# A hybrid MLA and RWKV-7 layer with routed experts: first loads moved a stage early, a folded tail tile, transposed experts of 96 rows, and the slot table made by matmuls

## The reference, cut to what matters

```python
h = rmsnorm(x); p = h @ w_in           # latents | rope key | RWKV columns z (1792) | gate logits (2*1024)
o_a = chunk_causal_attention(q, k, v)  # 8 heads, 96 wide, values 64 wide
o_b = rwkv7_time_mix(z, ...)           # 8 heads of 64: state S = S*w + (S a) b + v k
x = x + sum_n sigmoid(gate_n) * (branch_n @ w_out[n])
h2 = rmsnorm(x)
g = argmax_group(h2); e1, e2 = top2 experts of g     # 4 groups of 8 experts
x = x + sum_k weight_k * ((silu(h2 @ w_gate[e]) * (h2 @ w_up[e])) @ w_down[e])   # D 1024, FF 256
```

## Time and profile before

| | us |
|---|---|
| median of 3 runs (1848.87 to 1853.21) | 1850.72 |
| the profiled execution | 1846.78 |
| its span, first to last instruction | 1845.0 |
| PE busy in it | 1605.4 (87%) |
| DVE / ACT / POOL busy | 883.4 / 450.8 / 110.0 |
| mean granted TensorE clock, as a share of 2.4 GHz | 0.946 |

### The profile page before, as it was taken

How to read it: one execution, slowest core, us unless ns; L and a number is a source line. 1 busy time by engine, 2 the same in 40 slices (tenths; PEclk the granted TensorE clock), 3 DMA queues, 4 the chain that set the end, 5 groups by cost and what they waited for, 6 DMA issues and landing times. The chain is left out here.

```text
span 1845.0 us, 30700 instructions
## 1 busy us (share of the span) xinstructions
PE 1605.4 (87%) x12312; PEld 1037.5 (56%) x12312; DVE 883.4 (48%) x1874; ACT 450.8 (24%) x873; POOL 110.0 (6%) x131
## 2 busy tenths in 40 slices
PE   4999999659999999999994888759981599999994
PEld 3888888525666666666663555525540244444442
DVE  2454645536566666666663666526663122222221
ACT  2222222222222322332211333324540011111110
POOL 0000000000000000000000000000003222222221
PEclk9999999879999999999995999979995799999997
DMA  9322321262231231221104344244526499999982
GB/s 330 118 85 80 113 97 63 83 227 74 71 118 58 78 111 48 78 78 53 59 24 132 102 88 88 64 177 161 201 85 237 148 368 368 365 365 373 373 296 38
DMA packets 103630, 280.20 MB, mean 152 GB/s; under 512 B 31776, under 2 KB 50336, under 8 KB 94032
## 3 DMA queue, kind: packets, MB, share of 16 engines
q1 hardware_dynamic: 93680, 244.78, 37.6%
q0 software_dynamic: 9824, 33.63, 7.2%
HBM read 209.45 MB, written 68.98 MB: 151 GB/s over the span
## 5 line engine op out<-in xcount | busy, mean ns | idle before, releaser
L1069 PE MATMUL b_ps<-b_wg,b_hT 128*128 128x512 f32 x576 | 277.7, 615 | 29.6 <-DMA b_wg<-w_gates 29.3
L1986 PE MATMUL f_hidden<-wgu,f_xT 128*128 128x512 f32 x512 | 225.7, 594 | 0.0
L505 PEld LDWEIGHTS a_ps<-a_hT,a_wz 128*128 128x128 f32 x1792 | 202.6, 192 | 3.8 <-issue 3.8
L505 PE MATMUL a_ps<-a_hT,a_wz 128*128 128x128 f32 x1792 | 204.0, 275 | 0.0
L1069 PEld LDWEIGHTS b_ps<-b_wg,b_hT 128*128 128x128 f32 x576 | 101.4, 191 | 124.7 <-issue 119.9
L1986 PEld LDWEIGHTS f_hidden<-wgu,f_xT 128*128 128x128 f32 x512 | 97.7, 191 | 122.5 <-issue 122.5
L1753 PE MATMUL d_ps<-wo,d_oT 128*128 128x512 f32 x288 | 130.8, 603 | 0.8 <-DVE d_oT L1588 0.8
L2003 PE MATMUL f_down<-wd,f_midT 128*128 128x512 f32 x256 | 116.9, 600 | 1.0 <-DVE f_midT L2023 1.0
L1422 PE MATMUL c_score<-c_kT,c_qT 96*128 96x512 f32 (+2 forms) x192 | 76.2, 508 | 24.5 <-DMA c_v<-v_d 24.5
L2023 DVE COPY f_midT<-f_midps 128x256 f32<-128x256 f32 x32 | 13.6, 425 | 162.7 <-PE f_midps L1993 162.7
L1753 PEld LDWEIGHTS d_ps<-wo,d_oT 128*128 128x128 f32 x288 | 53.4, 192 | 59.4 <-issue 57.8
(11 more groups left out here) (308 smaller groups left out, 2474.6 us busy)
## 6 DMA issues: line engine op xcount, KB each, us to landing
wgu<-w_gate_up SPq DMA_DIRECT2D x32, 2048.0 KB, 13.7
wd<-w_down SPq DMA_DIRECT2D x32, 1024.0 KB, 6.7
b_hT<-hT_d SPq DMA_DIRECT2D x36, 512.0 KB, 4.1
gate_d<-b_logits SPq DMA_DIRECT2D x36, 256.0 KB, 2.6
d_gate<-gate_d SPq DMA_DIRECT2D x9, 1024.0 KB, 5.8
b_wg<-w_gates SPq DMA_DIRECT2D x4, 2048.0 KB, 12.7
zm_d<-a_zm SPq DMA_DIRECT2D x9, 896.0 KB, 4.6
b_zm<-zm_d SPq DMA_DIRECT2D x9, 896.0 KB, 6.5
```

What stands on the lines that cost most here:

```text
L505: mm = pe.matmul(banks[Z_BANKS[n % 2]][:, j * P:(j + 1) * P], wz[:, i, (g + j) * P:(g + j + 1) * P], hT[t % 2][:, i, :], start=(i == 0), s ...
L1069: mm = pe.matmul(banks[FILL][:], hT[q % 2][:, k, :], wg[u % 2][:, k, :], start=(k == 0), stop=(k == DC - 1))
L1986: mm = pe.matmul(hidden[b][:], xT[b][:, k, :], wgu[wb][:, k, :], start=(k == 0), stop=(k == DC - 1))
```

## The change

1. The first loads of a stage are issued by SP in the stage before it, into memory that is kept apart for them: mixing's constants, first zm, hT and gate weights during inputs; attention's first head during mixing; merge's constants and first tile (but the attention output) during attention; the first 3 experts' weights during merge. WB is 5.
2. The folded tail: the gate logits of the last tile use only its 32 real rows, as four matmuls of 32 stationary and 128 moving columns side by side (`QUADS`), in two parts for each unit in place of eight. `FILL_OF` and the fill of s = -1 are changed with it.
3. In mixing, `right_side`, `outputs` and `state` work in halves of 64 stationary columns; `state` computes only the diagonal blocks.
4. Attention takes the tiles in the order 7, 0, 6, 1, 5, 2, 4, 8, 3.
5. merge builds a 96-row table of token numbers and weights with two matmuls per tile, and gathers the first two experts' rows itself. The stage `slots` is gone; the DRAM table is left for overflow alone and is made during the experts' loop, on DVE (eight parts) and POOL (18 indirect DMAs).
6. `CAP` is 96. `up` has the weights as the stationary operand in halves of 64 columns and the rows as 96 moving columns, so its product is already turned and `turn_mid` is gone. OVERFLOW goes from 16 to 22 rounds.

```diff
-CAP = P
+CAP = 96
 OVERFLOW = 2 * (SEQ + DEC) // CAP
-WB = 4
+WB, WB_EARLY = 5, 3
+EARLY = 2
@@ inputs_stage, SP
+            def load_for_mixing():
+                sp.wait_ge(h_stored[0], 16)
+                sp.wait_ge(h_stored[1], 16)
+                sp.wait_ge(zm_stored, 16)
+                for dst, src in mixing_consts(early, io):
+                    sp.dma_start(dst, src).then_inc(early["consts_in"], 16)
+                sp.dma_start(early["zm"][0], io["zm_d"][0]).then_inc(early["zm_in0"], 16)
+                sp.dma_start(early["hT"][0][:], io["hT_d"][0]).then_inc(early["hT_in0"], 16)
+                sp.dma_start(early["wg"][0][:], io["w_gates"][:, :, 0:512]).then_inc(early["wg_in0"], 16)
...
+                if t == NT - 3:
+                    load_for_mixing()
@@ mixing
-        FILL_OF = (3, 2, 3, 3, 3, 2, 4, 4, 2, 1, 2, 3)
+        FILL_OF = (2, 2, 3, 2, 3, 2, 3, 4, 2, 1, 2, 2)
+        QUADS = [slice(DEC * n, DEC * n + DEC) for n in range(P // DEC)]
+        FOLDED = UW // len(QUADS)
+        parts_of = lambda q: DC if tile_of(q) < LAST else 2
...
-            return 2 if s < 0 else FILL_OF[k]
+            return 3 if s < 0 else FILL_OF[k]
@@ mixing, PE, fill
+                        for n, rows in enumerate(QUADS):
+                            mm = pe.matmul(banks[FILL][rows, 0:FOLDED], hT[q % 2][:, k, 0:DEC], wg[u % 2][:, k, n * FOLDED:(n + 1) * FOLDED],
+                                           start=(k == 0), stop=(k == DC - 1), tile_position=(0, DEC * n))
@@ right_side (outputs alike)
-                    pe.matmul(banks[XD][:, p * P:(p + 1) * P], art[t % 2][:, p, 0:P], S[t % 2][:, p, :], start=True, stop=False)
+                    for q in HALVES:
+                        pe.matmul(banks[XD][q, p * P:(p + 1) * P], art[t % 2][:, p, 0:P][:, q], S[t % 2][:, p, :], start=True, stop=False)
@@ state
-                    pe.matmul(banks[XD][:, cols], tok[t % 2][0:real, 1, cols], W[0:real, cols], start=True, stop=False)
+                    for q, cols in heads:
+                        pe.matmul(banks[XD][q, cols], tok[t % 2][0:real, 1, cols], W[0:real, cols], start=True, stop=False)
@@ mixing, SP, s == LAST
+                    load_head(sp, io, early, 0, 0, early["head_in0"])
@@ attention
-        tile_of = lambda p: p % STEPS
+        TILE_ORDER = (NPT - 1, 0, NPT - 2, 1, NPT - 3, 2, NPT - 4, NPT, 3)
+        tile_of = lambda p: TILE_ORDER[p % STEPS]
...
+            for dst, src in ((begun["ident"][:], io["ident"]), (begun["wr"][:], io["w_router"]), (begun["br"][:], io["b_router"].partition_broadcast(P)),
+                             (begun["before"][:], io["causal"][:, 0:P]), (begun["g_ffn"][:], io["norm_ffn_g"].partition_broadcast(P)),
+                             (begun["count_up"][:], io["count_up"].partition_broadcast(P)), (begun["real"][:], io["real"]), (begun["token"][:], io["token"]),
+                             (begun["places"][:], io["places"].partition_broadcast(P)), (begun["nobody"][:], io["nobody"])):
+                sp.dma_start(dst, src).then_inc(keep["begun_in"]["consts"], 16)
+            sp.dma_start(begun["gate0"][:], io["gate_d"][0]).then_inc(keep["begun_in"]["gate"], 16)
@@ merge, SP
+                if 1 <= t <= WB_EARLY:
+                    e = t - 1
+                    sp.dma_start(keep["wgu"][e][:], io["w_gate_up"][ORDER[e]]).then_inc(keep["weights_in"][f"up_in{e}"], 16)
+                    sp.dma_start(keep["wd"][e][:], io["w_down"][ORDER[e]]).then_inc(keep["weights_in"][f"down_in{e}"], 16)
@@ merge, POOL
+            pool.wait_ge(rows_known, 1)
+            for e in range(EARLY):
+                pool.tensor_copy(index[e][:], row_of[:, ORDER[e]:ORDER[e] + 1]).then_inc(index_set, 1)
...
+                pool.indirect_dma_start(xg[e][:], None, io["h2_d"].rearrange("t p n -> (t p) n"),
+                                        bass.IndirectOffsetOnAxis(ap=index[e][:, 0:1], axis=0)).then_inc(keep["gathered"][f"x_in{e}"], 16)
@@ merge, DVE, record
+                if n >= 1:
+                    dve.tensor_tensor(table[:], table[:], banks[7][0:CAP, P:P + 2 * NE], ALU.add)
...
+                dve.tensor_tensor(at_place[:], spread(places[:].unsqueeze(1), [P, 2, CAP]),
+                                  spread(rec[:, 2 * NE + 2:2 * NE + 4].unsqueeze(2), [P, 2, CAP]), ALU.is_equal)
+                dve.tensor_scalar(told[:, :, 0, :], hot(n), token[:, n:n + 1], None, ALU.mult)
+                dve.tensor_tensor(told[:, :, 1, :], hot(n), spread(rec[:, 2 * NE + 4:].unsqueeze(2), [P, 2, NE]),
+                                  ALU.mult).then_inc(told_ready, 1)
@@ merge, PE
+            def place_rows(n):
+                pe.wait_ge(told_ready, n + 1)
+                for k in range(2):
+                    mm = pe.matmul(banks[7][0:CAP, P:P + 2 * NE], at_place[:, k, :], told[:, k], start=(k == 0), stop=(k == 1))
@@ experts, up
-            for k in range(DC):
-                mm = pe.matmul(hidden[b][:], xT[b][:, k, :], wgu[wb][:, k, :], start=(k == 0), stop=(k == DC - 1))
+            for part, flag in enumerate(("gate_done", "up_done")):
+                bank = (gated, upped)[part][b]
+                for f in range(FB):
+                    cols = slice(f * CAP, (f + 1) * CAP)
+                    for k in range(DC):
+                        for half in HALVES:
+                            mm = pe.matmul(bank[half, cols], wgu[wb][:, k, (part * FB + f) * P:(part * FB + f + 1) * P][:, half],
+                                           xT[b][:, k, :], start=(k == 0), stop=(k == DC - 1))
+                mm.then_inc(s[flag], 1)
@@ experts, PE
-                turn_mid(pe, s, e)
                 if e + 2 < NE:
-                    turn(pe, s, e + 2, e % 2, e // 2 + 1)
-                project(pe, s, e, e % WB, e // WB)
+                    turn(pe, s, e + 2, (e + 2) % AHEAD, (e + 2) // AHEAD)
+                project(pe, s, e, e % 2, e % WB, e // WB)
@@ experts, POOL
                 if e + AHEAD < NE:
-                    gather(pool, s, e + AHEAD, e % AHEAD, (e + AHEAD) % (2 * AHEAD), ORDER[e + AHEAD])
+                    gather(e + AHEAD)
+                if 0 <= e - 10 < 2 * NT:
+                    scatter(e - 10)
```

More of the change, by code:

```diff
@@ L561, in _, with mixing @@
                 turn_heads(t)
-def mixing(nc, io):
+def mixing(nc, io, early):
     LEVELS = (2, 4, 8, 16, 32, 64)
@@ L1910, in experts @@
-def experts(nc, io, keep):
-    BLOCKS = NE + OVERFLOW + 2
+            pe.wait_ge(counted, NT)
+            place_rows(NT - 1).then_inc(table_done, 1)
+def experts(nc, io, keep):
+    TRASH = 2 * NT
+    BLOCKS = OVERFLOW + TRASH
+    NBMAX = -(-(SEQ + DEC) // CAP)
     AHEAD = 4
-    ORDER = [g * EPG + e for e in range(EPG) for g in range(NG)]
+    FB = FF // P
+    HALVES = (slice(0, P // 2), slice(P // 2, P))
     with ExitStack() as c:
@@ new lines, in experts @@
+        run, route = keep["run"], keep["route"]
+        slot = sb("slot", [CAP, OVERFLOW, 2])
+        oindex = sb("oindex", [CAP, 1], I32)
+        weight = sb("weight", [CAP, 1])
+        count_up = sb("count_up", [P, NE])
+        trash = sb("trash", [P, NT, 2])
+        token = sb("token", [P, NT])
+        more = sb("more", [P, NE])
+        bounds = sb("bounds", [P, NBMAX - 1])
+        gt = sb("gt", [P, NE, NBMAX - 1])
+        upto = sb("upto", [P, NE])
+        one = sb("one", [P, NE])
@@ new lines, in experts @@
+        base = sb("base", [P, NE])
+        owned = sb("owned", [P, OVERFLOW, NE])
+        q = sb("q", [P, NT, 2])
+        ge = sb("ge", [P, NT, 2, NBMAX - 1])
+        hb = sb("hb", [P, NT, 2, NE])
+        bb = sb("bb", [P, NT, 2])
+        over = sb("over", [P, NT, 2])
+        place = sb("place", [P, NT, 2])
+        entry = sb("entry", [P, NT, 2, 2])
+        cell = [[sb(f"cell{t}_{k}", [P, 1], I32) for k in range(2)] for t in range(NT)]
+        planf = sb("planf", [P, OVERFLOW + 1])
+        plan = sb("plan", [P, OVERFLOW + 1], I32)
@@ L2001, in project @@
             for h in range(2):
-                for k in range(2):
-                    mm = pe.matmul(down[h][:], midT[:, k, :], wd[wb][:, k, 512 * h:512 * h + 512], start=(k == 0), stop=(k == 1))
+                for k in range(FB):
+                    mm = pe.matmul(down[h][0:CAP, :], midT[b][:, k, :], wd[wb][:, k, 512 * h:512 * h + 512], start=(k == 0), stop=(k == FB - 1))
             mm.then_inc(s["down_done"], 1)
@@ L2073, in work @@
                 goes_on(pool, o["add_seen"])
-            pool.wait_ge(slot_in, 16 + START)
-            for e in range(AHEAD):
-                gather(pool, s, e, e, e, ORDER[e])
+            for e in range(EARLY, AHEAD):
+                gather(e)
+            pool.memset(one[:], 1.0).then_inc(one_set, 1)
             for e in range(NE):
```

556 lines of the change are left out of this document (280 added, 276 removed).

## The result

The changed kernel takes 1759.42 us in the median (1758.26 to 1761.13), 0.9506 of before (95% interval 0.949 to 0.9523). The prediction was 1669, with a range from 1634 to 1716: the sign was right, the gain was 91 us where 182 were forecast. The profiled execution spans 1756.4 us, 88.6 less than before.

The account below looks back on a forecast made before the run. The prediction took PE's own work to bound mixing and experts, PE's waits attention, with idle gaps between stages; its terms summed to -181 us, 1846.8 to 1665.8, as a median 1669, range 1634 to 1716.

Parts of the forecast that it names:

- A: Start of mixing: with loads issued during inputs, PE's first matmul comes earlier, -16 us.
- C: Start of attention: with the first head loaded during mixing, PE starts earlier, -6 us.
- E: Start of merge: with constants and first tile already loaded, PE starts earlier, -15 us.
- B: Body of mixing: less fill, and halves side by side in outputs, right_side and state, -45 us.
- D: Attention's tile order: wide next to narrow tiles gives ACT time and cuts PE's waits, -10 us.
- G: Between merge and experts: no slots stage and gathers issued in merge bring PE's first turn earlier, -41 us.
- H: The experts: PE's period falls to 9.73 us with the other work hidden, -56 us.
- R1: Rival in the experts: DMA, not PE, sets the pace, costing 10 to 25 us; chance 22%.
- R2: Rival: DVE's chain takes PE's savings in mixing and attention's order gains nothing, +43 us; chance 12%.
- R3: Rival in the experts' up: a fixed time per instruction bounds small matmuls, +42 us; chance 3%.
- R4: Rival in experts and mixing: the halves don't run side by side, +208 us, slower than before; chance 4%.
- R5: Rival in the experts: an expert overflows its 96 rows and one overflow block runs, about +33 us; chance 4%.

Follow-up runs that it names:

- e3: The changed kernel with mixing's fill batches never running over the end of a unit, same number of matmuls; 1737.83 us, ratio 0.9396.
- e4: The changed kernel with attention's tiles taken in the order 0 to 8 again; 1755.15 us, ratio 0.949.
- e8: The changed kernel with the first two gathers issued at the start of the experts, not in merge, and the identity kept in memory; 1759.73 us.
- e1: The changed kernel with the experts' gathers issued one period earlier, before POOL waits for the output rows; 1738.85 us, ratio 0.94.
- e9: The changed kernel with gathers two periods early, fill ending at unit ends, attention's tiles in order and the identity kept; 96-row gathers and scatters; 1715.18 us.
- e11: The four edits of e9 on the changed kernel, with 128 rows in the gathers and 96 in the scatters; 1690.6 us, ratio 0.914.
- e12: The changed kernel with gathers of 128 rows as the only edit, scatters and PE still at 96; 1736.48 us, ratio 0.9376.
- e7: The changed kernel with gathers a period early and the scatter of each expert's output rows left out; 1698.39 us.
- e5: The kernel before the change, with half of the experts' up and down matmuls left out; 1841.72 us.
- e10: The four edits of e9 on the changed kernel, with 128 rows in both gathers and scatters; 1721.09 us, ratio 0.9303.

## Why the prediction was wrong, step by step

**A, C, E, F, I** are right within 2 us each. (For E, the first DMA of merge before was issued at 1199.11, not at 1199.49; nothing hangs on it.)

**B**: the terms are right, the sum missed one. In the timeline an outputs pair now takes 0.69 us (forecast 0.68), right_side 0.45 (0.46), state 1.08 where 0.92 was forecast. With e3's schedule the body is 544.4 us, 44.7 less than before, against -45. The prediction saw in fill only PE's cover for DVE's answers, and put no price on where its batches end. The old FILL_OF added up to eight at every end of a unit; 28 a step doesn't, and each crossing waits for ACT to empty the only bank of fill.

**D**: "Wide next to narrow gives ACT time" holds, the -10 doesn't: I asked nowhere who is late next, which is DVE (e4).

**G**: 5 us short. I took 3.7 us for the meeting, and it took 8.8. By e8 3 of these 5 us belong to the gathers in flight; the other 2 stay open.

**H**, the step that failed: that PE at 9.73 us an expert sets the pace and the gathers land within a budget. PE's period was right to 0.1 us (9.68), but the experts took 376.4 us where 317.8 were forecast, 44.7 of it waits and the rest PE's own work at the lower clock that followed them. R1, DMA at the pace, had 22%, but at a price of 10 to 25 us where it took 59. Three things were wrong in how the prediction weighed this.

- The round trip. "Inside its budget of 13.4 us against 11.1" has no row behind it, and it doesn't hold for the new period. Before, 14.2 us lay between a gather and its turn (1603.23 to 1617.45). Two shorter periods take 3.3 of that away and leave 11, which the 11.1 of before uses up. The landing became 14.5. e1, with no wait for gathers, takes 356.5 us for this part: so 20 of the 59 are the round trip's.
- The rate. "Rows of 96 rather than 128" stood against R1 and spoke for it: gathers of 96 rows slow the weight loads (e9, e11, e12). The rate is 336 GB/s, under the lowest of R1's own sum (345), and at it 116 MB take 345 us, 29 more than the 316 of PE there. With 128 rows in gathers that are issued two periods early (e11) the part takes 329.2.
- The scatters, whose cost R1 took by bytes. Without them, and with gathers a period early, the part takes 317.1 us, as forecast (e7).

"The 370 is only what PE's period asked for" was nearer to the truth than e5's 354 suggests, since 128-row gathers moved 377 and 385 in e10 and e11. But it said nothing on traffic with 96 rows.

The Trainium skill's 358 GB/s (HBM Reference, Specifications), which I set aside, isn't a ceiling here: e11 moved 385. The section itself gives 358 as a core's share when both cores of a pair stream, and says that a core streaming alone gets well above it, with which the 385 agrees. The 11.0 us an expert that I worked out from it would have been nearer to the outcome than mine, by luck, for the reason is another.

**R2** came in half: attention gained nothing. Its other half did not, since mixing is held up by ACT's copies of the logits and not by DVE's chain (e3). **R3, R4, R5** didn't come: halves run side by side (2.69 us for 16 pairs of 96 columns, 0.168 a pair), and no overflow round did work.

## What to carry to other kernels

An engine at 100% isn't the only bound where DMA's share is also at 1. Before an engine is made faster, take work out of it and see whether the time follows: e5 would have told that, with gathers issued where they are, PE's 5 us an expert were worth next to nothing. Read such a run with its clock, since an engine that is left idle may run slower. Work out anew, for the new period, how long each transfer may take: a budget shrinks with the period. And a gather with fewer than 128 rows may cost more than it saves. Here padding rows were cheap in the gathers and dear in the scatters.

When a resource has one buffer, the schedule that feeds it must end its batches where the buffer changes hands. A hand-written list of counts carries such alignments without saying so.

## What the runs showed that I had not expected

- Beside gathers of 96 or 112 rows and scatters the core's DMA moves 336 to 349 GB/s, with weight loads that are unchanged. With gathers of 128 rows it is 364 to 385.
- A wait of PE costs more than its length: in the experts of the changed kernel PE is busy 15 us longer than in e11 with the same matmuls, at a lower clock after waits.
- Scattering 128 rows instead of 96 (e10 for e11) costs 30 us, though the rate is still 377 GB/s for 385: the landing of a scatter goes from 18.8 to 21.3 us, and two y buffers don't cover that.
- The version with gathers of 128 rows two periods early, aligned fill and a kept identity takes 1690.6 us, 0.914 of before and faster than either kernel. Its tile order is the old one. What holds it now is the scatter's landing or DMA's rate: DVE waits for y, but its period of 10.5 us is also just what 4.06 MB take at 385 GB/s. More y buffers were not tried.
